# Score products of the differential attention: four padded products per map pair, or eight 32-row products in two row groups

## The reference

```python
def _diff_attend(q, k, v, lam):
    scale = DA_DK ** -0.5                  # DA_DK = 32
    k1, k2 = k[..., 0, :], k[..., 1, :]
    def block(qb):                         # Q_BLOCK = 128 queries
        s1 = jnp.einsum('bqhd,bkhd->bhqk', qb[..., 0, :], k1).astype(jnp.float32) * scale
        s2 = jnp.einsum('bqhd,bkhd->bhqk', qb[..., 1, :], k2).astype(jnp.float32) * scale
        p = jax.nn.softmax(s1, axis=-1) - lam * jax.nn.softmax(s2, axis=-1)
        return jnp.einsum('bhqk,bkhd->bqhd', p.astype(v.dtype), v)
    return _map_query_blocks(block, q)
```

## Time and profile before

| | |
|---|---|
| median of three runs | 3359.14 us |
| profiled execution, own time | 3356.46 us |
| its span | 3354.9 us |
| PE busy | 3043.6 us, 91% |
| DVE busy | 992.2 us, 30% |
| ACT busy | 814.4 us, 24% |
| POOL busy | 644.2 us, 19% |
| TensorE clock granted, mean | 0.962 of 2.4 GHz |
| differential attention, layer 0 | starts at about 671, ends at about 804 us of the span |
| differential attention, layer 1 | starts at about 2313, ends at about 2446 us |

### The profile page before, as it was taken

The page is one execution under the profiler, slowest core; times in us unless marked ns, Lnnn a source line. Parts: engine busy times, 40 slices in busy tenths (PEclk is TensorE's granted clock), DMA queues, the critical chain, the costliest instruction groups (busy, mean ns, idle before and its releaser), DMA issues.

```text
span 3354.9 us, 56818 instructions
## 1 busy us (share of the span) xinstructions
PE 3043.6 (91%) x23500; PEld 2515.6 (75%) x23500; DVE 992.2 (30%) x1978; ACT 814.4 (24%) x1220; POOL 644.2 (19%) x392
## 2 busy tenths in 40 slices
PE   6998989768999989999998988986799998999997
PEld 3656964446888889999956588544488887999997
DVE  1334721464121221111142266125521211211111
ACT  2113112343111141222220220223421112422222
POOL 0001100031222223333300020001222222333331
PEclk8899999999999999999998999989999999999999
DMA  6000001001333222222220100100023332222221
GB/s 257 26 25 26 4 28 44 1 2 39 117 113 113 93 84 88 94 88 94 88 91 7 51 3 3 49 21 2 1 85 113 120 117 84 78 86 94 88 94 69
DMA packets 55007, 224.42 MB, mean 67 GB/s; under 512 B 6336, under 2 KB 6496, under 8 KB 53824
## 3 DMA queue, kind: packets, MB, share of 16 engines
q1 hardware_dynamic: 53568, 206.67, 17.9%
q0 software_dynamic: 1280, 15.48, 1.2%
HBM read 218.56 MB, written 3.57 MB: 66 GB/s over the span
## 4 chain that ended last, share of the span: by engine, by line
PE 87%; DVE 7%; issue 3%; ACT 2%; DMA 1%; SPq 0%; DVEq 0%; POOL 0%; ACTq 0%; POOLq 0%
PE ps_dense L661 44%; PE ps_dense L651 13%; PE ps_aux L1315 4%; PE ps_aux L1152 3%; PE ps_dense L1163 2%; PE ps_aux L675 2%; PE ps_dense L1174 2%; PE ps_aux L934 2%; PE ps_aux L926 2%; DVE arena L2187 2%; PE ps_aux L914 2%; PE ps_dense L688 1%; PE ps_aux L755 1%; PE ps_dense L797 1%; DMA w_ring<-in_w_early 1%
## 5 line engine op out<-in xcount | busy, mean ns | idle before, releaser
L624 POOL TENSOR_TENSOR w_low<-w_ring,w_high 128x1024 fp32r<-128x1024 f32 x208 | 514.9, 2476 | 1263.3 <-ACT w_high L1422 1262.5
L661 PE MATMUL ps_dense<-h_high,w_high 128*128 128x320 f32 x2048 | 478.3, 315 | 18.8 <-DVE h_low L1783 18.8
L661 PE MATMUL ps_dense<-h_low,w_high 128*128 128x320 f32 x2048 | 468.0, 310 | 0.0
L661 PE MATMUL ps_dense<-h_high,w_low 128*128 128x320 f32 x2048 | 467.7, 310 | 0.0
L651 PE MATMUL ps_dense<-h_norm,w_ring 128*128 128x512 f32 (+1 forms) x1536 | 429.6, 441 | 15.4 <-ACT h_norm L1443 7.5
L651 PEld LDWEIGHTS ps_dense<-h_norm,w_ring 128*128 128x128 f32 x1536 | 238.0, 194 | 208.2 <-issue 195.6
L1422 ACT ACTIVATE w_high<-w_ring 128x1024 fp32r<-128x1024 f32 x208 | 219.3, 1055 | 656.0 <-PE ps_dense L661 442.9
L661 PEld LDWEIGHTS ps_dense<-h_high,w_high 128*128 128x128 f32 x2048 | 340.1, 189 | 24.7 <-issue 18.9
L661 PEld LDWEIGHTS ps_dense<-h_low,w_high 128*128 128x128 f32 x2048 | 344.1, 189 | 0.0
L661 PEld LDWEIGHTS ps_dense<-h_high,w_low 128*128 128x128 f32 x2048 | 343.7, 189 | 0.0
L661 PE MATMUL ps_dense<-z_high,w_high 128*128 128x320 f32 x1280 | 296.5, 313 | 14.2 <-DVE mod_a L1766 14.2
(11 more groups left out here) (327 smaller groups left out, 3320.2 us busy)
## 6 DMA issues: line engine op xcount, KB each, us to landing
w_ring<-in_w_mlp SPq DMA_DIRECT2D x128, 512.0 KB, 3.3
w_ring<-in_w_gate SPq DMA_DIRECT2D x64, 640.0 KB, 3.9
w_ring<-in_w_late SPq DMA_DIRECT2D x64, 512.0 KB, 4.6
w_ring<-in_w_early SPq DMA_DIRECT2D x48, 512.0 KB, 3.4
w_ring<-in_w_in SPq DMA_DIRECT2D x48, 512.0 KB, 3.3
w_ring<-in_w_out SPq DMA_DIRECT2D x16, 512.0 KB, 3.3
arena<-in_dft POOLq DMA_DIRECT2D x2, 3776.0 KB, 13.6
par<-in_par POOLq DMA_DIRECT2D x3, 1667.0 KB, 7.5
```

What stands on the lines that cost most here:

```text
L624: g.tensor_tensor(w_low[:, n % 2], ring[:, slot, 0:KC, :], w_high[:, n % 2].bitcast(F32), ALU.subtract).then_inc(w_low_in.sem, 1)
L661: last = mm(psD[:, b, s * 512:s * 512 + HALF], w_[:, par_, k, :], x_[:, k, s * HALF:(s + 1) * HALF], start=k == 0 and x_ is x_high and w_ ...
```

## The change

The padded query buffer, POOL's 40 copies a layer into it, and the semaphores for it are taken out; POOL's `h_low` subtractions stay. The queries of a map are now read from their own 32 partitions of `d_q`, and the keys from the same 32 partitions of `d_k`, so that the two maps of a head use two different groups of 32 rows of the TensorE array. Both maps' scores are issued by one call, in turn: map 0 with 512 keys, map 1 with 512 keys, map 0 with 128 keys, map 1 with 128 keys. The one call stands where the score of map 1 stood, behind `values(u - 2)`. It waits for the exponentials of both maps before its first product. DVE's and ACT's programs are not changed.

```diff
-                g.memset(q_pad, 0.0).then_inc(q_zero.sem, 1)
-                held(pool, *q_zero.nth(l, 1))
-                held(pool, *d_rot_in.nth(l, 4))
-                for u in range(U):
-                    hh, t = divmod(u, NT)
-                    if u >= 2:
-                        held(pool, *s_ps.nth(l, U + 2 * (u - 1)))
-                    for m in range(2):
-                        g4 = hh * 2 + m
-                        rows = slice(32 * (g4 % 4), 32 * (g4 % 4) + 32)
-                        last = g.tensor_copy(q_pad[rows, g4 % 4, t % 2], d_q[rows, g4 // 4, t * P:(t + 1) * P])
-                    last.then_inc(q_padded.sem, 1)
-                    if 2 <= u < 2 + KC:
-                        c = u - 2
-                        held(pool, *q_padded.nth(l, u + 1))
-                        held(pool, *h_high_in.nth(l, c + 1))
-                        g.tensor_tensor(h_low[:, c], h[:, c], h_high[:, c].bitcast(F32), ALU.subtract)\
-                            .then_inc(h_split.sem, 1)
-                        held(pool, *h_split.nth(l, c + 1))
+                for c in range(KC):
+                    held(pool, *h_high_in.nth(l, c + 1))
+                    g.tensor_tensor(h_low[:, c], h[:, c], h_high[:, c].bitcast(F32), ALU.subtract)\
+                        .then_inc(h_split.sem, 1)
+                held(pool, *h_split.nth(l, KC))
...
-                def score(u, maps=range(n_maps)):
+                def score(u):
                     hh, t = divmod(u, NT)
-                    if n_maps == 2:
-                        pe.wait_ge(*q_padded.nth(l, u + 1))
-                    for m in maps:
-
+                    for m in range(n_maps):
                         if n_maps == 1 and u >= 2:
                             pe.wait_ge(*exps.nth(l, u - 1))
                         if n_maps == 2 and u >= 1:
-                            pe.wait_ge(*exps.nth(l, U + 2 * u - 1 + m))
-                        b2 = 2 * (u % 2) if n_maps == 1 else 2 * m
-                        out = psA[:, b2:b2 + 2, :].rearrange("p b n -> p (b n)")
-                        qt, k = scores(hh, m, t)
-                        if t < NT - 1:
-                            for a, b in SEGS:
-                                last = mm(out[:, a:b], qt, k[:, a:b], start=True, stop=True)
-                        else:
-                            last = mm(out[:, 0:CTX], qt, k[:, T:KEYS], start=True, stop=True)
-                        last.then_inc(s_ps.sem, 1)
+                            held(pe, *exps.nth(l, U + 2 * u - 1 + m))
+                    for a, b in SEGS if t < NT - 1 else ((0, CTX),):
+                        for m in range(n_maps):
+                            b2 = 2 * (u % 2) if n_maps == 1 else 2 * m
+                            out = psA[:, b2:b2 + 2, :].rearrange("p b n -> p (b n)")
+                            qt, k = scores(hh, m, t)
+                            keys = k[:, a:b] if t < NT - 1 else k[:, T:KEYS]
+                            last = mm(out[:, a:b], qt, keys, start=True, stop=True)
+                            if b != LAT:
+                                last.then_inc(s_ps.sem, 1)
...
                         turn(u - 1)
-                        if u + 1 < U:
-                            score(u + 1, (0,))
                         if u >= 2:
                             values(u - 2)
                         if u + 1 < U:
-                            score(u + 1, (1,))
+                            score(u + 1)
...
-                pe.wait_ge(*d_rot_in.nth(l, 4))
-                pe.wait_ge(*dv_in.nth(l, 3))
+                held(pe, *d_rot_in.nth(l, 4))
+                held(pe, *dv_in.nth(l, 3))
 
                 def scores(hh, m, t):
                     g4 = hh * 2 + m
-                    return q_pad[:, g4 % 4, t % 2], d_k[:, g4 // 4]
+                    lanes = slice(32 * (g4 % 4), 32 * (g4 % 4) + 32)
+                    return d_q[lanes, g4 // 4, t * P:(t + 1) * P], d_k[lanes, g4 // 4]
```

More of the change, by code:

```diff
@@ L277, in trunk @@
         d_osq = d_vf
-        q_pad = cv(4, 2, P)
         d_small = cv(8, 20)
@@ L410, in trunk @@
         br_done = signal("differential_branch_done", 1)
-        q_zero = signal("q_zeroed", 1)
-        q_padded = signal("q_padded", U)
         lam_sum = signal("lam_sum", 1)
@@ L597, in _ @@
                 held(pool, *pv_in.nth(l, U))
-                g.memset(q_pad, 0.0).then_inc(q_zero.sem, 1)
-                held(pool, *q_zero.nth(l, 1))
-                held(pool, *d_rot_in.nth(l, 4))
-                for u in range(U):
-                    hh, t = divmod(u, NT)
-                    if u >= 2:
-                        held(pool, *s_ps.nth(l, U + 2 * (u - 1)))
-                    for m in range(2):
-                        g4 = hh * 2 + m
-                        rows = slice(32 * (g4 % 4), 32 * (g4 % 4) + 32)
-                        last = g.tensor_copy(q_pad[rows, g4 % 4, t % 2], d_q[rows, g4 // 4, t * P:(t + 1) * P])
-                    last.then_inc(q_padded.sem, 1)
-                    if 2 <= u < 2 + KC:
-                        c = u - 2
-                        held(pool, *q_padded.nth(l, u + 1))
-                        held(pool, *h_high_in.nth(l, c + 1))
-                        g.tensor_tensor(h_low[:, c], h[:, c], h_high[:, c].bitcast(F32), ALU.subtract)\
-                            .then_inc(h_split.sem, 1)
-                        held(pool, *h_split.nth(l, c + 1))
+                for c in range(KC):
[3 more added lines that the diff above has]
+                held(pool, *h_split.nth(l, KC))
                 held(pool, *stored.nth(l, 3))
                 held(pool, *stored_kv.nth(l, 2))
-                held(pool, *q_padded.nth(l, U))
                 def low_part(l, n, slot, more=0):
```

## The result

The changed kernel takes 3486.89 us (median of 4 runs, 3480.74 to 3492.38), against 3359.23 us for the kernel before on the same chip (median of 4, 3358.96 to 3365.41). The ratio is 1.0379, with a 95% interval of 1.0363 to 1.0396. The forecast said slower, and it is slower, but by 128 us where the forecast had 77. The time lies above the whole range, 7 us beyond its upper end and 20 us above rival two.

The account below looks back on a forecast made before the run. The changed stage was taken as a round trip between PE and DVE. A layer: 119.7 + 26.7 - 107.0 - 1.0 = +38.4 us; two layers +76.8, giving 3436 us, range 3380 to 3480.

Parts of the forecast that it names:

- rival two: Second attention: half clock throughout, since 32-row products do not lift it; 42 instead of 26.7 us a layer, 3467 us, chance 0.11.
- The order on PE: Second attention: with both scores behind the values, PE and DVE hide nothing of each other; a full step 7.40 us.
- DVE's part: Second attention: DVE's stretch from the awaited score to the next turn, its instructions unchanged, 4.07 us a step.
- The full-clock sum of a full step: Second attention, turn to turn: 0.69 + 1.24 + 1.4 + 4.07 = 7.40 us, against 6.03 before.
- S, the pair: Second attention: time of the paired 32-row scores until DVE reads them, 1.4 us, from DeltaNet's 64-row products.
- rival three: Second attention: the row groups do not overlap, paired scores take 2.2 us; 3466 us, chance 0.11.
- The start: Before the first turn: scores no longer wait for POOL's first copy but wait for both exponentials; gain 1.0 us a layer.
- POOL: Second attention: POOL's subtraction falls into DVE's idle time and no longer slows its combine; if not, 2.9 us a layer return.
- The clock: Second attention: PE idles over 4 us a step, one clock fall in each of 17 steps, 26.7 us a layer.
- the forecast sum: Second attention, first to last turn at full clock, all full and short steps added: 119.7 us a layer.
- the high end: Upper limit of the clock term in the second attention: every piece at 1.2 GHz, about 42 us a layer.
- The stages outside unchanged: Profile after, outside the second attention: the other stages were to stay as they were, with no term in the sum.

Follow-up runs that it names:

- e3: The changed kernel with eight unread 256-column products over 128 rows behind each score to fill PE's idle time: 3408.45 us against 3353.14, ratio 1.0166.
- e2: The kernel before with its 128-row padded products, both scores moved behind the values: 3427.22 us against 3353.14, ratio 1.0227.
- e1: The changed kernel with PE's old order and split by maps put back, 32-row products kept: 3465.18 us against 3353.14, ratio 1.0333.
- e4: The changed kernel with eight unread 256-column products over 32 rows behind each score: 3526.72 us against 3353.14, ratio 1.0525.
- e7: The changed kernel with scores ahead of the turn, both reductions ahead of the combine, both exponentials ahead of ACT's copy: 3321.77 us against 3358.41, ratio 0.9900.
- e10: The changed kernel itself measured again on another chip beside the kernel before: 3484.66 us against 3357.11, ratio 1.0382.
- e8: The kernel before, 128-row padded products kept, with scores ahead of the turn and DVE and ACT reordered to match: 3305.24 us, ratio 0.9844.
- e9: e8 with three places for padded queries instead of two: 3306.44 us against 3357.11 for the kernel before, ratio 0.9856.
- e11: e9 with POOL's `h_low` subtractions moved two units later: 3294.43 us against 3360.43 for the kernel before, ratio 0.9811.
- e12: e11 with scores read from 64 of the padded rows instead of 128: 3311.47 us against 3360.43 for the kernel before, ratio 0.9869.
- e6: The changed kernel with the pair of 32-row scores ahead of the values: 3411.57 us against 3358.41, ratio 1.0162.
- e5: The changed kernel with eight unread 256-column products over 64 rows behind each score: 3417.98 us against 3358.41, ratio 1.0180.

## Why the prediction was right and wrong

**The order on PE: right.** The forecast said that nothing would hide anything any more. The values stand directly behind the turn, the first reduction directly behind the scores (745.45 against an end at 745.41), and the turn behind the copy. DVE's part was forecast at 4.07 us. It is 4.15 in the step shown, and PE's wait of 4.08 before its turn at 739.34 is as long. The full-clock sum of a full step was forecast at 7.40; e3 measured 7.30 to 7.46. That the order alone makes the kernel slower is shown by e2. It is not the only reason why the direction came out right: the rows alone would have made it slower too (e1). One reading of the prediction is off without consequence: the two reads of PSUM are 1.67 of DVE's 4.07 us, four tenths and not half. The chain through the step before the one shown (its values are short) reads as the forecast wrote it, only with PE at half clock:

```profile
730.87 1.32 PE ps_dense L1153 x5
732.20 0.62 PE ps_dense L1142 x2
732.82 2.49 PE ps_aux L1132 x8
735.30 0.82 DVE arena L2165
736.59 0.56 DVE arena L2183
737.97 0.83 DVE arena L2165
738.92 0.29 DVE arena L2191
```

**S, the pair: right.** Forecast 1.4 us, measured 1.38 at full clock (from the scores at 700.33 to DVE's reduction at 701.71). DeltaNet's 64-row pairs were a fair guide to 32-row pairs, and rival three is refuted. The Trainium skill agrees: "TensorE: Matmul & The Clock Gate", Part 3, has products in different row groups run side by side.

**The start: the sign right, the gain under half of the forecast.** Forecast was a gain of 1.0 us a layer. Measured from the stage's first rotation to the first turn it is 0.8 in layer 0 and 0.1 in layer 1. The wait of the scores for POOL's first copy is gone, and what is left is the wait for the rotation:

```profile
679.20 2.13 PE L1132 MATMUL ps_aux<-arena 32*128 32x512 f32 x8 [2.13 <-DVE arena L2218]
```

**POOL: right.** Its subtraction runs at 740.70 for 1.54 us, in DVE's idle stretch, and L2183 takes 0.54 to 0.56 us in the full steps shown, no longer beside it. (It does still meet POOL's L606 at 754.79 and takes 1.03 us there.)

**The clock: wrong, and this is the step that failed.** "I therefore count one fall in each of 17 steps: 17 x 1.57 = 26.7 us a layer." A fall, as in the kernel before, is followed by a return within the step. Here there is hardly a return: in layer 0 no turn runs at full clock, five value products take 2.22 us or more, and the scores of five steps come back wholly or in part (1.35 to 1.97 us), four of them behind a wait of at most 3.6 us. The granted clock was forecast at 0.7 to 0.8 and is 0.55. Measured against the forecast sum, the term is 159.9 - 119.7 = 40.2 us, close to the 42 of the high end ("every piece at 1.2 GHz"). The mechanism is that of rival two. The prediction had its row, the 32-row rotations at a granted 0.50 with PE busy 5.64 of 6.07 us, and even said what it might mean. It then gave that case 0.11, because it took idle time to be what lowers the clock. e1 and e4 refute that: no long idle stretch, and still 0.52 and 0.57 in the stage.

**The end of the stage: left out.** The forecast kept everything behind the last turn as it was. But the clock is still low there, and the products of L1270, on 128 rows, run at it: 4.63 us instead of 2.43.

```profile
849.91 2.82 PE L1142 MATMUL ps_dense<-arena 128*64 128x128 f32 x12
854.42 4.63 PE L1270 MATMUL ps_aux<-arena,con 128*128 128x512 f32 x8 [1.69 <-ACT arena L1668]
858.71 0.88 PE L643 MATMUL ps_dense<-h_high,w_high 128*128 128x320 f32 x2
```

That is 3.55 us a layer. "The stages outside unchanged" was wrong for this reason, and for one more: it put two terms at nothing.

**Outside the stage: 11.9 us, in part unexplained.** Of these, 9.2 us are a wait that the kernel before does not have at all. The wait list of PE for the whole run of the changed kernel (us in total, times, longest):

```profile
PE ps_dense L643 <- DVE x_res L2274: 9.2, 6, 1.7
```

It stands in the MLP, whose code was not touched. All seven experiments built from the changed kernel's code have it (e1, e3 to e7, e10: 6.4 to 9.9 us), and none of the five built from the kernel before does (e2, e8, e9, e11, e12). The first kind also moves more on the instruction queue: 172 to 176 packets and 2.8 to 2.9 MB, against 117 or 118 packets and 1.9 MB. The two go together in every trace, but no run separates them. What causes the wait is open; that code is loaded late would be a guess.

**The account.** The forecast for a layer was +38.4. To it come 13.5 for the clock (40.2 instead of 26.7), 3.55 for the end, 0.6 for the start and some 6 outside: 62.0, and the span grew by 62.0 a layer. So the forecast missed mostly by the clock, 27 us in two layers. The range missed by the two terms put at nothing: its upper end, 3480, lies 13 us above the case of the clock at half throughout (3467), and what the forecast kept unchanged outside the stage, with the start, came to 20 us.

## What to carry to other kernels

Before moving a product across a round trip between two engines, ask what each piece hides: here the place of the value products alone was worth 32 us a layer (e6). Price a product by the rows it uses as well as by its columns, and look at the granted clock of the nearest stage with that few rows. The padded products cost copies on an engine with time to spare, and some waits for them (7.9 us in layer 0 of e8); the 32-row ones brought the stage's clock to near half, and a low clock is paid for by every piece of the stage and by what follows it. Where a stage is a round trip, issue the request for the next unit before the answer to this one (e8, e11): that was worth 1.6 to 1.9%, while the pairing, whose products really do run side by side, lost to the padded products in both orders in which the two were compared (e10 with e2, e7 with e8). Without the unexplained wait outside, the second loss is small: 9.2 us in the two stages.

## What the runs showed of the hardware

- PE can be busy without a break and stay at 1.2 GHz: 20.00 of 20 us at a granted 0.50 with the stage's scores and the fill on 32 rows (e4). Over the stage the clock is 0.57 there; with fill on 128 rows it is 0.97 (e3), on 64 rows 0.90 to 0.94 (e5). That the turns and values on 128 rows between them do not lift it was not expected.
- Scores on 64 rows in a dense stage gave 0.88, low twice a layer (e12), against 1.00 with 128 rows (e11). What sets the time of these two is open.
- What counts is the rows that a product uses, not those with values in them: of the padded queries' 128 rows 96 are zeros, and the stage's clock with them is 1.00 (e8), where 32-row products in the same order have 0.70 and 0.81 (e7).
- Two 32-row groups issued in turn into different banks overlap fully: eight records in 1.35 us, the time of four.
- With 128-row products, idle stretches of 3 us in each step gave a clock of 0.77, with full-clock and half-clock steps in the same layer (e2).
